# A ring of 18 expert slots instead of 16, and what moves with it

## What is computed

```python
def expert_choice_ffn(xn, w_router, w_gate, w_up, w_down):
    cap = CAPACITY_FACTOR * S // N_EXPERTS
    aff = jax.nn.softmax(jnp.einsum('bsd,de->bse', xn, w_router).astype(jnp.float32), axis=-1)
    top_aff, top_idx = lax.top_k(jnp.swapaxes(aff, 1, 2), cap)
    xg = xn[bidx, top_idx]
    hid = jax.nn.silu(jnp.einsum('becd,edf->becf', xg, w_gate)) * jnp.einsum('becd,edf->becf', xg, w_up)
    y = jnp.einsum('becf,efd->becd', hid, w_down) * top_aff[..., None].astype(xn.dtype)
    return jnp.zeros((B, S, D), dtype=y.dtype).at[bidx, top_idx].add(y)
...
    h = h + expert_choice_ffn(rmsnorm_2(h, norm_ffn[l]), w_router[l],
                              w_exp_gate[l], w_exp_up[l], w_exp_down[l])
    ple_gate = jax.nn.sigmoid(rmsnorm_2(h, norm_ple[l]) @ w_ple_gate[l])
    h = h + ple_gate * (p[l] @ w_ple[l])
return rmsnorm_2(h, norm_final)
```

## Time and profile before

| | us |
|---|---|
| median of 3 executions | 2022.86 |
| lowest, highest of them | 2020.67, 2023.09 |
| span of the profiled execution | 2021.3 |

### The profile page before, as it was taken

One profiled execution on the slowest core, in us unless ns is written; L12 is line 12 of the kernel. 1 busy time (PEld: TensorE's weight loads), 2 busy tenths in 40 slices (PEclk: granted clock), 3 DMA queues, 4 the chain that ended last, 5 costly groups with the idle time before them and its releaser, 6 DMA issues.

```text
span 2021.3 us, 23284 instructions
## 1 busy us (share of the span) xinstructions
PE 1936.9 (96%) x9434; PEld 1409.0 (70%) x9434; DVE 787.5 (39%) x1191; ACT 553.9 (27%) x1120; POOL 998.1 (49%) x568
## 2 busy tenths in 40 slices
PE   7999999999999999999999999999999999999988
PEld 6878887678788888887866768887864444434436
DVE  2444658551423301433544374555241212212133
ACT  4534437432421200211132333342131000000025
POOL 5786775757377878887644477446700000000012
PEclk9989999999999999999999999999999999999999
DMA  5321113323123333322311123112779999999982
GB/s 182 99 67 32 43 49 110 123 73 97 50 84 94 94 95 101 96 94 84 125 55 53 53 62 94 53 53 84 273 273 422 421 421 421 421 422 421 421 360 73
DMA packets 92698, 335.81 MB, mean 166 GB/s; under 512 B 7697, under 2 KB 9489, under 8 KB 67761
## 3 DMA queue, kind: packets, MB, share of 16 engines
q1 hardware_dynamic: 88864, 321.29, 43.4%
q10 hardware_dynamic: 3584, 12.52, 1.7%
q0 software_dynamic: 144, 0.52, 0.1%
HBM read 328.01 MB, written 6.29 MB: 165 GB/s over the span
## 4 chain that ended last, share of the span: by engine, by line
PE 77%; DMA 7%; POOL 7%; DVE 4%; ACT 3%; issue 1%; SPq 0%; PEldq 0%; ACTq 0%; DVEq 0%; PEld 0%; POOLq 0%
PE bank L609 47%; PE bank L1827 11%; DMA arena<-in_w_exp_up 3%; PE bank L1858 3%; POOL shared_r L667 2%; PE bank L786 1%; DMA shared<-in_w_exp_up 1%; DMA arena<-in_w_exp_gate 1%; DMA arena<-in_w_exp_down 1%; POOL shared_r L649 1%; PE bank L630 1%; POOL shared_r L648 1%; PE bank L1496 1%; PE bank L1845 1%; PE bank L1509 1%
## 5 line engine op out<-in xcount | busy, mean ns | idle before, releaser
L609 PE MATMUL bank<-shared_r 128*128 128x512 f32 (+1 forms) x3888 | 911.7, 389 | 16.1 <-POOL shared_r L667 6.7
L609 PEld LDWEIGHTS bank<-shared_r 128*128 128x128 f32 x3888 | 703.2, 190 | 179.4 <-issue 27.0
L648 POOL TENSOR_TENSOR shared_r<-shared,small 128x1024 fp32r<-128x1024 f32 (+1 forms) x172 | 336.0, 1954 | 871.6 <-DMA shared<-in_w_ple_gate 493.6
L649 POOL TENSOR_TENSOR shared_r<-shared,shared_r 128x1024 fp32r<-128x1024 f32 (+1 forms) x172 | 424.2, 2467 | 13.5
L1827 PE MATMUL bank<-shared,arena 128*64 128x512 f32 x768 | 170.8, 594 | 9.5 <-DMA shared<-in_w_exp_gate 3.2
L1827 PE MATMUL bank<-arena 128*64 128x512 f32 x768 | 170.5, 595 | 9.7 <-DMA arena<-in_w_exp_up 3.8
L609 PE MATMUL bank<-shared_r,arena_r 128*128 128x512 f32 x768 | 176.1, 391 | 0.0
L609 PEld LDWEIGHTS bank<-shared_r,arena_r 128*128 128x128 f32 x768 | 144.2, 188 | 31.5
L667 POOL TENSOR_TENSOR shared_r<-shared,shared_r 128x1024 fp32r<-128x1024 f32 x40 | 101.4, 2536 | 95.0 <-ACT shared_r L658 95.0
L1827 PEld LDWEIGHTS bank<-shared,arena 128*64 128x64 f32 x768 | 57.4, 137 | 116.9 <-issue 106.7
L1827 PEld LDWEIGHTS bank<-arena 128*64 128x64 f32 x768 | 56.0, 137 | 117.2 <-issue 103.3
(11 more groups left out here) (423 smaller groups left out, 2121.7 us busy)
## 6 DMA issues: line engine op xcount, KB each, us to landing
shared<-in_w_in SPq DMA_DIRECT2D x80, 512.0 KB, 3.6
arena<-in_w_exp_gate SPq DMA_DIRECT2D x32, 1024.0 KB, 25.5
shared<-in_w_exp_gate SPq DMA_DIRECT2D x32, 1024.0 KB, 25.6
shared<-in_w_exp_up SPq DMA_DIRECT2D x32, 1024.0 KB, 23.4
arena<-in_w_exp_up SPq DMA_DIRECT2D x32, 1024.0 KB, 24.1
arena<-in_w_exp_down SPq DMA_DIRECT2D x32, 1024.0 KB, 25.6
shared<-in_w_exp_down SPq DMA_DIRECT2D x32, 1024.0 KB, 26.0
shared<-in_w_up SPq DMA_DIRECT2D x32, 512.0 KB, 3.7
```

Source lines behind the costliest of these rows:

```text
L609: ins = pe.matmul(dst, W_, x_, start=first, stop=final)
L648: link(pool.tensor_tensor(hi, raw(p), small[:, 18:19].to_broadcast([P, hi.shape[1]]), ALU.add))
L649: pool.tensor_tensor(lo, raw(p), hi.bitcast(F32), ALU.subtract).then_inc(S_("w_split"), 1)
```

## The change

The program reserves 1024 bytes per partition for GpSimd's DMA descriptors instead of the default, the arena shrinks by 192 floats, and behind X comes a new tensor `spare` of 2 x 2048 floats per partition: two more slots. They stand first in the ring, which now has 18 slots, and the order in which the panels of the first round wait is written anew: q = 0 and 1 (spare) for nothing, 2 to 7 for ygla, 8 and 9 (under the raw parts) for the last split before `late`, 10 to 13 for out2, 14 and 15 for the router, 16 and 17 for the ple products. GpSimd's one DMA goes to SP, ahead of the first part of `xout`, with its wait. The parts of ple_gate get other places: raw ones `inner[6:8]`, splits the spare slots and `inner[2:6]`; they are issued ahead of p_keep's way back. The new `slots_over` waits for the last use of a slot: for slot 0 the last panel is q = 180, so x_used 91; for slot 16 q = 178, 90; for slot 2 q = 182, 92. SQF moves to `shared[2 * PANEL:3 * PANEL]`.

```diff
@@ -33,10 +33,10 @@
 NE = 16
 CAP = 2 * S // NE
 PAIRS = NE // 2
-RING = 16
+RING = 18
 XPANEL = 2048
 PANEL = 4096
-ARENA = 26960
+ARENA = 26768
 NEG = -1.0e30
 
 
@@ -94,6 +94,9 @@
 
     arena_r = nc.alloc_sbuf_tensor_at("arena_r", [P, ARENA], F32R, offset=arena_at)
     X = sb("X", [P, ST, D])
+    spare_at = -(-nc.sbuf_base // 32) * 32
+    spare = sb("spare", [P, 2 * XPANEL])
+    spare_r = nc.alloc_sbuf_tensor_at("spare_r", [P, 2 * XPANEL], F32R, offset=spare_at)
 
     shared_at = -(-nc.sbuf_base // 32) * 32
     shared = sb("shared", [P, 4 * PANEL])
@@ -244,13 +247,19 @@
 
     def raw(p):
 
-        return shared[:, 2 * PANEL + 1024 * (p % 4):2 * PANEL + 1024 * (p % 4) + parts[p]["kp"] * parts[p]["n"]]
+        of, at, n = shared, 2 * PANEL + 1024 * (p % 4), parts[p]["kp"] * parts[p]["n"]
+        if p >= late:
+            of, at = arena, ring_at + 6 * XPANEL + 1024 * (p % 4)
+        return of[:, at:at + n]
 
     def split_slot(p):
 
         at, n = 3 * PANEL + 2048 * (parts[p]["split"] % 2), parts[p]["kp"] * parts[p]["n"]
-        if p >= late + 2 and (p - late) % 6 >= 2:
-            at = ring_at + XPANEL * (4 + (p - late) % 6 - 2)
+        if p >= late and (p - late) % 6 < 2:
+            at = XPANEL * ((p - late) % 6)
+            return spare_r[:, at:at + n], spare_r[:, at + n:at + 2 * n]
+        if p >= late:
+            at = ring_at + XPANEL * ((p - late) % 6)
             return arena_r[:, at:at + n], arena_r[:, at + n:at + 2 * n]
         return shared_r[:, at:at + n], shared_r[:, at + n:at + 2 * n]
 
@@ -1427,8 +1436,9 @@
     PICK = Area(oht_at).take(ST, NE)
     ring_at = a.at
     inner = [a.take(XPANEL) for _ in range(8)]
+    spares = [spare[:, i * XPANEL:(i + 1) * XPANEL] for i in range(2)]
     outer = [shared[:, i * XPANEL:(i + 1) * XPANEL] for i in range(8)]
-    ring = inner[0:6] + outer[4:8] + outer[2:4] + outer[0:2] + inner[6:8]
+    ring = spares + inner[0:6] + outer[4:8] + outer[2:4] + outer[0:2] + inner[6:8]
     assert len(ring) == RING
     out2 = [BASE["out2a"] + j for j in range(4)] + [BASE["out2b"] + j for j in range(4)]
     ple = [BASE["ple_a"] + j for j in range(3)] + [BASE["ple_b"] + j for j in range(2)] + [BASE["ple_c"] + j for j in range(3)]
@@ -1437,7 +1447,7 @@
     PTT = inner[7][:, D:2 * D].rearrange("p (k s) -> p k s", k=2)
     PS_ = [arena[:, hidt_at + 512 * i:hidt_at + 512 * i + 512] for i in range(6)] + [bc[:, 512 * i:512 * i + 512] for i in range(2)]
     PP = arena[:, ring_at:ring_at + ST * D].rearrange("p (i j d) -> p i j d", i=2, j=ST)
-    SQF = arena[:, ring_at + 2 * XPANEL:ring_at + 4 * XPANEL].rearrange("p (i j d) -> p i j d", i=2, j=ST)
+    SQF = shared[:, 2 * PANEL:3 * PANEL].rearrange("p (i j d) -> p i j d", i=2, j=ST)
     PG = Area(ST * D).take(ST, D)
 
     def xpv(pe, h):
@@ -1802,6 +1812,11 @@
     def x_rows(e):
         return slice(64 * e, 64 * e + 64)
 
+    def slots_over(eng, slot):
+
+        q = slot + (2 * 4 * 3 * PAIRS - 1 - slot) // RING * RING
+        eng.wait_ge(S_("x_used"), q // 2 + 1)
+
     def expert_load(sp, q):
 
         e, c, w, i = q % 2, q // 2 % 4, q // 8 % 3, q // 24
@@ -2021,8 +2036,6 @@
         hg_pool(pool, link)
         mix_pool(pool, link)
         rest("out1", 0)
-        bank_written(pool, cell_out(H - 1, ST - 1))
-        pool.dma_start(bc[:, 0:D], A["norm_final"].partition_broadcast(P)).then_inc(S_("nf_in"), 16)
         for name in ("xqkv", "xout", "up0", "down0", "up1", "down1"):
             rest(name, 0)
         rest("proj_a", 0)
@@ -2712,21 +2725,28 @@
         sp.dma_start(pos_i, A["positions_2"].rearrange("a (j p) -> p (a j)", p=P), allow_slow_non_contiguous=True).then_inc(S_("sink_in"), 16)
         sp.dma_start(WG[:, :, :], A["g_weights"].rearrange("p (k n) -> p k n", k=KT)).then_inc(S_("wg_in"), 16)
         for p in range(4, late):
+            if p == panels[PB["xout"]]["parts"][0]:
+                bank_written(sp, cell_out(H - 1, ST - 1))
+                sp.dma_start(bc[:, 0:D], A["norm_final"].partition_broadcast(P)).then_inc(S_("nf_in"), 16)
             load(p)
-        bank_done(sp, BASE["ygla"] + 7)
         for q in range(2 * 4 * 3 * PAIRS):
-            if q == 6:
+            if q == 2:
+                bank_done(sp, BASE["ygla"] + 7)
+            if q == 8:
+                sp.wait_ge(S_("w_split"), parts[late - 1]["split"])
+            if q == 10:
                 bank_written(sp, out2[7])
-            if q == 12:
+            if q == 14:
                 bank_done(sp, BASE["router"])
-            if q == 14:
+            if q == 16:
                 bank_written(sp, ple[7])
             expert_load(sp, q)
-        sp.wait_ge(S_("x_used"), (2 * 4 * 3 * PAIRS - RING + 2) // 2)
-        sp.dma_start(PP[:, :, :, :], p_keep.rearrange("p (i j d) -> p i j d", i=2, j=ST)).then_inc(S_("pp_in"), 16)
-        sp.wait_ge(S_("x_used"), (2 * 4 * 3 * PAIRS - RING + 10) // 2)
+        slots_over(sp, 0)
+        slots_over(sp, 16)
         for p in range(late, late + 4):
             load(p)
+        slots_over(sp, 2)
+        sp.dma_start(PP[:, :, :, :], p_keep.rearrange("p (i j d) -> p i j d", i=2, j=ST)).then_inc(S_("pp_in"), 16)
         for p in range(late + 4, len(parts)):
             load(p)
         y = out.rearrange("a (j p) d -> p (a j) d", p=P)
@@ -2758,7 +2778,7 @@
     from concourse import mybir as _mybir
     from concourse.bass_utils import run_bass_kernel_spmd as _run
 
-    nc = _bacc.Bacc("TRN2", target_bir_lowering=False, num_devices=1)
+    nc = _bacc.Bacc("TRN2", target_bir_lowering=False, num_devices=1, dynamic_dma_scratch_size=1024)
     arrays, args = {}, {}
     for name in _INS:
         a = _np.ascontiguousarray(inputs[name])
```

## The result

| | before | after |
|---|---|---|
| median of 20 executions, us | 2020.32 | 2015.68 |
| lowest, highest | 2015.86, 2024.50 | 2013.23, 2019.50 |
| span of the profiled execution | 2021.3 | 2013.5 |

The ratio after/before is 0.9976, with a 95% interval from 0.9969 to 0.9984: faster by 4.8 us on 2020.3, between 3.2 and 6.3 (the two medians lie 4.64 us apart). The two profiled executions lie 7.8 us apart, which is more. To see why, the span is cut at two points that both kernels have: the start of the first expert matmul, and the start of the last 16 of them, which wait for the last panel.

A forecast was written before the change was run, and what follows sets the result against it. The prediction took the expert panels' DMA stream at 421 GB/s as the bound. Its terms, -4.98 (ring) and 0 for opening, norm_final and tail, gave -5.0 us: span 2016.3, median 2017.9 us, range 2015.6 to 2021.2.

The forecast's parts named there:

- What is the bound: Expert stage: the unbroken panel stream at 421 GB/s sets the end, not TensorE, though PE fills most of the chain.
- (1) The ring, -4.98: Expert panels: 18 slots hold 18 MiB instead of 16 at the first release, leaving 174 panels to load, 4.98 us gained.
- (2) The opening, 0: Before the experts: panels 8 and 9 wait for the last split, 6.4 us earlier; worth margin, between 0 and 0.5 us.
- (3) norm_final, 0: Moving its issue from GpSimd to SP, ahead of the first w_xo part: gain 0, cost at most 0.70 us.
- (4) The end, 0 in bounds of -1.1 and +0.7: Last gate product: parts issued 11.7 us earlier, ahead of p_keep, gain nothing, as the first part is not late now.
- The seam's 1.11 us: First gate matmul at 1966.81 us, held 1.11 us by VectorE; gained only if that hung on GpSimd's work beside VectorE's.
- rival C: More than the ring: the seam gives back 1.11 us and some overlap goes, gain 6.1 us or more, 2016.8; chance 0.08.
- Rival A: Ring fill does not help in full: half gives 2.5 us, 2020.4, none 2022.9; variant: TensorE becomes the bound; chance 0.19.
- Rival B: Gate parts get ahead of the last panels, delaying them 6.8 us: net +1.8, 2024.7; chance 0.05.
- The slack of TensorE, 21.4 us: Last expert pair: at its own pace TensorE would end at 1937.8 us, but it ends at 1959.2.
- The upper end of the range, 2021.2: Whole run: A at half, with the scatter of the fastest or slowest run.
- the 1.6 us between span and median: Whole run: median of three runs, 2022.86, lies 1.6 us above the profiled span; kept, turning span 2016.3 into 2017.9.

The follow-up runs named there:

- ring16: The kernel after with the ring back to 16 slots, spare slots holding only gate parts: stage 447.84 us against 442.60; whole run 2020.43 us, ratio 1.0003.
- ring14: The kernel after with a ring of 14 slots, the last two of the arena also taken out: stage 452.57 us, median 2025.07 us, ratio 1.0025.
- parts_ahead: ring16 with the gate product's first four parts issued ahead of the last eight panels: stage 452.88 us, 5.04 more than ring16; median 2026.31 us.
- open_late: The kernel after with panels 8 and 9 waiting for out2's last bank instead of the last split: stage 442.63 us against 442.60, ratio to before 0.9975.
- nf_on_gpsimd: The kernel after with norm_final's broadcast back on GpSimd: stage 442.75 us, median of three runs 2015.55 us.
- late_order: The kernel after with p_keep's way back ahead of the gate parts, as before: stage 442.85 us, tail 65.79 us, ratio 0.9984.
- half_panels: The kernel after loading only the first half of each panel's columns from panel 18 on: stage 428.15 us, no wait for a panel.
- clock_fill2: The kernel after with unread matmuls in four TensorE idle gaps, two sets placed ahead of the transposes: median 2012.55 us, ratio to before 0.9962.

## Why the prediction was right or wrong

**What is the bound: right.** The DMA stream from the first release on; ring16, ring14 and parts_ahead each move the end by their bytes over 421 GB/s (4.98 us), within 0.3 us.

**(1) The ring, -4.98: right.** Measured in the stage -4.87 by the two first profiles, -5.24 against ring16, -4.7 for the pair of slots before it. By the 358 GB/s of the Trainium skill ("DMA: Bandwidth & Descriptors", section "Bandwidth") the step would have been 5.9 us; the stream ran at 421 in all profiles with whole panels, and the step was 4.7 to 5.2. The same section gives the 358 for a core whose neighbour streams, too, and has 425 GB/s for 16 MB on a core that streams alone; here one core runs the program, and the trace agrees with that figure.

**(2) The opening, 0: right**, with open_late at +0.03. **(3) norm_final, 0: right** by nf_on_gpsimd. **(4) The end, 0 in bounds of -1.1 and +0.7: right**, late_order +0.25 in the stage and +0.09 in the tail, no more than profiles of one kernel differ. The seam's 1.11 us belongs to VectorE, so rival C falls. The last panel was under way for 26.70 us, below the 27 that would have spoken against it.

**Rival A** falls: the ring was full with idle time to spare, and by half_panels TensorE had slack left. **Rival B** falls for the reason given, the order of the queue; its price was overstated, 6.8 us for what cost 5.04.

**The slack of TensorE, 21.4 us, was mis-sized:** 19.3 measured, by the two waits named above, 2.0 us together. It decided nothing. The upper end of the range, 2021.2, does not follow from its words either: half of rival A is 2020.4, and the slowest run lies 0.2 us, half the scatter 1.2 us above the median, which gives 2020.6 or 2021.6.

**The step that failed is the last one, from the sum to the time: the 1.6 us between span and median, "and I keep that".** I took the median of three runs, 2022.86, and the profiled span 1.6 us under it for the level of before, and subtracted. Over 20 runs before has a median of 2020.32, 1.0 us below that span. The 1.6 us are no property of the kernel: in every execution on record with its span the time is 1.7 to 1.8 us above its own span, so the profiled one, of 2021.3, was most likely the slowest of the three, 2023.09. The forecast 2017.9 is thus 2.2 us above the 2015.68 measured, about half of the effect itself, and measured from the level that before really has it says only -2.4 us, half of what came, while the sum of the parts was right (-4.98 against -4.87 in the stage). The profile held a warning that I did not use: the low clock near 140 us. The clock line of the page has an 8 in its third slice, and the stretch from 139 to 149 us stood at 0.55 in before. How long that slow stretch lasts is not the program's but the execution's (the same wait stood in all profiles), and a profile that has a long one of them is a slow sample. I had put the scatter between runs into the range by its width (1.2 us to each side) and not by where three samples may lie within it. That the measured median lies within 0.1 us of the lower end, 2015.6, on its inner side, is luck.

The chances named 0.2%, 4.05 us, as the border; the ratio is 0.24%, with an interval that reaches to both sides of it. With 20 runs the worth of the ring is seen by the total only just; by the stage, at once.

## What to carry to other kernels

Where a stage is bound by an unbroken stream of weights, what counts is how many bytes are in before the first buffer is released; each further buffer is worth its transfer time (here from 14 to 18 buffers), if the DMA engines have idle time ahead of the stage and the consumer slack behind it, and the order of filling is worth nothing once the ring is full in time. Cut a span at marks that both kernels share before you compare: a stage can be told to tenths of a microsecond where whole runs scatter by several. Before a forecast is set on the level of a few runs, look at the granted clock of the profile for slow stretches that another execution needn't have, and ask which of the timed runs the profile is.

## What the hardware showed that I had not expected

- Waits of TensorE of 2.2 to 2.6 us in a stage of small matmuls were followed in 33 of 40 cases by a granted clock of 0.5, for 3.4 us in most, 6.8 in four and 10.2 in one (before, near 140 us); in seven cases the same wait left the clock at 1.00. This can explain a part of the scatter of 2013 to 2020 us of one kernel: with the four gaps filled, six runs lay within 1.2 us. In the stream-bound stage waits of 1.2 to 1.5 us did not lower it in after (1.00 from 1511 to 1951 us), nor did one of 2.63 us near 1940 us in clock_fill2; the wait of 4.09 us in parts_ahead did (0.68 in the 4 us from 1944 on).
- SyncE's issue of a transfer can take many times longer than its shortest. A panel took some 0.5 us to issue at 1441 us in after and mostly 2.13 in the steady stream. The four gate parts took 8.29 us and p_keep, right behind them, 9.84; in before p_keep, right behind the last panel, took 2.13, and the four parts, 14.7 us later, 1.92. In after each landed 22 to 23 us later. So a queue full of panels alone is not what made p_keep's issue long; which part the gate parts in front of it have in that is not shown. Nothing waited behind them here, but an issuing engine with other work would have.
- Parts of 512 KiB in a full queue delayed the stream by 5.04 us for 2.1 MB, so they ran at about its 421 GB/s, though alone in a stretch they had reached only 90 GB/s at a share of 0.29. Why scaling that rate by the share gave too little (310 GB/s) is not shown.
